# A two-layer streaming encoder step: layers written out in place of a loop, and buffers handed back without TensorE drains

## The reference

```
for l in range(2):
    h = rmsnorm(x, norm1_g[l])
    xa, ga, xq, q, k, v, gates = split(h @ w_in[l])
    ya = rg_lru(causal_conv(xa)) * gelu(ga)            # mixer A, a recurrence
    yb = pooled(xq) @ pool_w[l]                        # mixer B
    yc = diff_attention(rotary(q), rotary(k), v)       # mixer C, 8 heads, two softmaxes each
    g = sigmoid(gates)                                 # three gates
    m = g0 * (ya @ proj_a[l]) + g1 * (yb @ proj_b[l]) + g2 * (yc @ proj_c[l])
    x = x + m @ w_out[l]
    h2 = rmsnorm(x, norm2_g[l])
    s = scores of (h2 @ peer_wq[l]) against sub-keys   # 8 heads, 2 x 128 keys
    idx, gate = 16 best pairs of keys, softmax         # out of 16384 experts
    act = gelu(<h2, u[idx]>)                           # one neuron per expert
    x = x + sum(gate * act * v[idx])
y = rmsnorm(x, final_g)
```

## Time and profile before

| | |
|---|---|
| median of 3 runs | 2577.77 us (2577.13 to 2579.86) |
| the profiled execution | 2582.31 us, span from the first to the last instruction 2580.6 us, 38213 instructions |
| busy share of the span | TensorE 77% (weight loads 44%), VectorE 62%, GpSimd 30%, ScalarE 26% |
| granted TensorE clock, mean | 0.909 |
| DMA | 852.67 MB, mean 330 GB/s |

### The profile page before, as it was taken

How to read it: one execution, slowest core, us unless ns; L and a number is a source line. 1 busy time by engine, 2 the same in 40 slices (tenths; PEclk the granted TensorE clock), 3 DMA queues, 4 the chain that set the end, 5 groups by cost and what they waited for, 6 DMA issues and landing times.

```text
span 2580.6 us, 38213 instructions
## 1 busy us (share of the span) xinstructions
PE 1992.8 (77%) x11708; PEld 1135.9 (44%) x11708; DVE 1587.4 (62%) x4310; ACT 673.0 (26%) x1659; POOL 779.6 (30%) x831
## 2 busy tenths in 40 slices
PE   7999997888677666566689999888786776656666
PEld 5555786655334212111255557866553442111112
DVE  3544046565767788787535440556667678777785
ACT  2422113331323222222223230233312132222223
POOL 0122012232434344444201210132334443444341
PEclk9999999999888788888899999999998988787878
DMA  6124649999999999999741348499999999999996
GB/s 212 64 102 166 242 166 404 418 411 419 418 419 403 409 420 418 413 410 416 306 153 64 135 155 283 169 404 418 409 418 417 420 403 409 420 407 413 411 421 251
DMA packets 156818, 852.67 MB, mean 330 GB/s; under 512 B 19312, under 2 KB 39280, under 8 KB 72640
## 3 DMA queue, kind: packets, MB, share of 16 engines
q0 software_dynamic: 95280, 677.24, 63.8%
q1 hardware_dynamic: 61328, 172.89, 18.1%
HBM read 843.35 MB, written 6.71 MB: 329 GB/s over the span
## 4 chain that ended last, share of the span: by engine, by line
PE 24%; DMA 24%; issue 15%; DVE 13%; PEld 12%; PEldq 5%; DVEq 3%; ACT 2%; POOL 1%; ACTq 0%; POOLq 0%; SPq 0%
DMA W<-in_peer_uv_dram,IDX 9%; DMA MIX_RINGS<-in_peer_uv_dram,IDX 9%; PE ps L766 7%; DMA WQKV_E<-in_peer_uv_dram,IDX 5%; PEld ps L836 5%; PEldq L1031 4%; PE ps L1045 4%; PEld ps L1029 3%; PE ps L784 3%; DVE MIX_RINGS L1603 3%; DVEq L1442 2%; PEld ps L901 2%; PE ps L772 2%; DVE W L1603 1%; PEld ps L864 1%
## 5 line engine op out<-in xcount | busy, mean ns | idle before, releaser
L1029 PE MATMUL ps<-MIX_RINGS,GC 64*64 64x512 f32 x3712 | 637.7, 689 | 201.7 <-ACT GC L1248 155.0
L711 POOL DMA_INDIRECT MIX_RINGS<-in_peer_uv_dram,IDX x400 | 429.7, 1074 | 797.0 <-PEq L1031 443.8
L1029 PE MATMUL ps<-W,GC 64*64 64x512 f32 x1840 | 388.6, 718 | 242.4 <-ACT GC L1248 221.5
L1029 PEld LDWEIGHTS ps<-MIX_RINGS,GC 64*64 64x64 f32 x3712 | 182.3, 152 | 517.5 <-issue 517.5
L711 POOL DMA_INDIRECT W<-in_peer_uv_dram,IDX x182 | 203.7, 1119 | 448.9 <-PEq L1031 372.8
L1248 ACT ACTIVATE GC<-twins,WV 128x64 f32<-128x64 f32 x640 | 170.5, 336 | 569.1 <-DVEq L1616 562.5
L1603 DVE CUSTOM_DVE_ANT_0 MIX_RINGS<-MIX_RINGS 128x1024 f32<-128x1024 f32 x224 | 268.4, 1223 | 74.3 <-DMA MIX_RINGS<-in_peer_uv_dram,IDX 67.1
L1603 DVE CUSTOM_DVE_ANT_0 MIX_RINGS<-MIX_RINGS,WQKV_E 128x1024 f32<-128x1024 f32 x176 | 213.0, 1225 | 161.6 <-DMA MIX_RINGS<-in_peer_uv_dram,IDX 154.2
L1029 PEld LDWEIGHTS ps<-W,GC 64*64 64x64 f32 x1840 | 105.7, 154 | 444.1 <-issue 444.1
L1242 ACT ACTIVATE GV<-AV 128x4 f32<-128x4 f32 x160 | 32.9, 205 | 710.9 <-DVEq L1604 710.9
L1603 DVE CUSTOM_DVE_ANT_0 W<-W,MIX_RINGS 128x1024 f32<-128x1024 f32 x126 | 154.0, 1225 | 42.5 <-DMA W<-in_peer_uv_dram,IDX 31.4
(11 more groups left out here) (265 smaller groups left out, 2748.0 us busy)
## 6 DMA issues: line engine op xcount, KB each, us to landing
W<-in_merge_w_dram SPq DMA_DIRECT2D x40, 1024.0 KB, 4.9
W<-in_merge_w_dram SPq DMA_DIRECT2D x60, 512.0 KB, 13.7
WQKV_E<-in_qkv_w_dram SPq DMA_DIRECT2D x16, 1536.0 KB, 7.4
W<-in_query_w_dram SPq DMA_DIRECT2D x16, 1024.0 KB, 11.5
W<-in_w_in_dram SPq DMA_DIRECT2D x12, 1024.0 KB, 10.7
W<-in_query_w_dram SPq DMA_DIRECT2D x20, 512.0 KB, 9.1
W<-in_out_w_dram SPq DMA_DIRECT2D x8, 1024.0 KB, 14.5
MIX_RINGS<-in_peer_uv_dram,IDX POOLq DMA_INDIRECT x400, 13.6
```

The lines of the kernel that those rows point to most:

```text
L711: pool.indirect_dma_start(UV[r], None, table, bass.IndirectOffsetOnAxis(IDX[:, n % 2, j:j + 1], 0))\
L1029: pe.matmul(ps[o:o + CHUNK, n:n + 512], w[r, :], v[r, d * 512:(d + 1) * 512], start=False, stop=False, skip_group_check=True)
```

## The change

The loop over the layers becomes a Python loop, so that both layers are written out one after the other and every target of a wait is a constant. The fillers `nop(nofuse=True)` behind waits are taken out on all engines. TensorE's drains that gave buffers back go, except the ones in `experts` and at the layer's end; in their place the last matmul of the group counts the semaphore up, and semaphores that then say the same thing twice are merged into one (`ga_ps`, `pa_ps`, `cb_ps`, `xb_ps`, `cache_free` go; others wait on `w_used`, `half_used`, `att_done`). Two things more: in `first_queries` half of the `wqh_used` counts is replaced by `pq_ps`; and the square of the first tile ahead of the second norm is taken in four quarters as the additions to X finish, with ScalarE's root table loaded ahead, and summed by VectorE. The order of TensorE's work is the same as before. The cut diff shows one place of each kind, in the order gate, branches, chunk, rest_queries, head, experts and ff for TensorE, then ScalarE and VectorE.

```
-            with sp.Fori(0, DEPTH) as l:
+            for l in range(DEPTH):
...
                 sp.wait_ge(*layer_done.at(l, 0))
-                sp.nop(nofuse=True)
...
                         h = g * 2 + par
-                        sp.wait_ge(*cache_free.at(l, h - 1))
-                        sp.nop(nofuse=True)
+                        if g:
+                            sp.wait_ge(*att_done.at(l, h - 1))
...
                                   start=c == 0, stop=c == KC - 1)
-                i.then_inc(ga_ps.sem, 1)
-                pe.drain().then_inc(w_used[b].sem, 1)
+                i.then_inc(w_used[b].sem, 1)
...
-                pe.drain().then_inc(w_used[3].sem, 1)
+                i.then_inc(w_used[3].sem, 1)
...
-                i.then_inc(pa_ps.sem, 1)
-                pe.drain().then_inc(w_used[4].sem, 1)
+                i.then_inc(w_used[4].sem, 1)
...
                             .then_inc(half_used[4].sem, 1)
-                    pe.drain().then_inc(cb_ps.sem, 1)
...
-                i.then_inc(pq_ps.sem, 1)
-                pe.drain().then_inc(w_used[slot].sem, 1)
+                i.then_inc(w_used[slot].sem, 1)
...
                 pe.wait_ge(*rot_done.at(l, 2 * (3 * g + 2 * par + 1)))
-                pe.nop(nofuse=True)
                 pe.wait_ge(*ex_done.at(l, h * 2 * TILES))
-                pe.nop(nofuse=True)
...
                 i.then_inc(att_done.sem, 1)
-                pe.drain().then_inc(cache_free.sem, 1)
...
                     pe.wait_ge(*dg_ready.at(l, p + 2))
-                    pe.nop(nofuse=True)
...
-                        i.then_inc(ff_ps.sem, 1)
-                    pe.drain().then_inc(w_used[FF_SLOT[u]].sem, 1)
+                        i.then_inc((ff_ps, w_used[FF_SLOT[u]])[k].sem, 1)
...
-                act.wait_ge(*xa_ev.at(l, GB))
-                squares([0])
+                act.activation(LE[:, 0:1], eps_c[:, :], ACT.Sqrt)
+                for n in range(GB):
+                    act.wait_ge(*xa_ev.at(l, n + 1))
+                    i = act.activation(HN[0][:, n * UNIT:(n + 1) * UNIT], X[:, 0, n * UNIT:(n + 1) * UNIT], ACT.Square,
+                                       accum_out=ssq[:, n:n + 1])
+                act.drain().then_inc(sqa_done.sem, 1)
+                act.wait_ge(*ssa_ready.at(l, 1))
+                act.activation(sd[:, 0:1], ss[:, 0:1], ACT.Sqrt, bias=eps_c[:, :], scale=1.0 / D_MODEL)\
+                    .then_inc(sq_done.sem, 1)
...
-                fence()
+                dve.wait_ge(*sqa_done.at(l, 1))
+                dve.tensor_reduce(ss[:, 0:1], ssq[:, :], AX_X, ALU.add)
+                dve.drain().then_inc(ssa_ready.sem, 1)
                 normed(l, 1, 0)
```

More of the change, by code:

```diff
@@ L272, in build @@
         ss = sb("ss", [P, TILES])
+        ssq = sb("ssq", [P, GB])
         sd = sb("sd", [P, TILES])
@@ L397, in build @@
         wqh_in = landing("wqh_in", 2 * (PH - AHEAD))
-        wqh_used = signal("wqh_used", 2 * (PH - AHEAD))
-        pq_ps = signal("pq_ps", Q_BLOCKS)
+        wqh_used = signal("wqh_used", PH - AHEAD)
+        pq_ps = signal("pq_ps", PH)
         pq_ev = signal("pq_ev", Q_BLOCKS)
@@ L430, in scores, with chunk_done @@
             return a if t < 2 else a[0:DEC_SEQ]
+        def chunk_done(l, c):
+            return half_used[(3, 4)[c % 2]].at(l, c // 2 + 1)
         def bcast(row):
@@ L709, in gathers @@
                         pool.wait_ge(*uv_free.at(l, PREV[p] + 1))
-                    pool.nop(nofuse=True)
                     pool.indirect_dma_start(UV[r], None, table, bass.IndirectOffsetOnAxis(IDX[:, n % 2, j:j + 1], 0))\
                         .then_inc(uv_in[r].sem, 16)
-            with pool.Fori(0, DEPTH) as l:
+            for l in range(DEPTH):
                 for h in range(HEADS):
@@ L794, in branches @@
                     for c in range(RC):
-                        pe.matmul(two(bank(3 + b, 0, UNIT)), YT[:, b * RC + c, 0:P], W2[3][:, :, b * RC + c, :],
-                                  start=c == 0, stop=c == RC - 1)
-                pe.drain().then_inc(w_used[3].sem, 1)
+                        i = pe.matmul(two(bank(3 + b, 0, UNIT)), YT[:, b * RC + c, 0:P], W2[3][:, :, b * RC + c, :],
+                                      start=c == 0, stop=c == RC - 1)
+                i.then_inc(w_used[3].sem, 1)
                 pe.wait_ge(*w_in_slot[4].at(l, FF_USES[4] + u + 1))
@@ L865, in rest_output @@
                                       W2[u % 2][:, :, c, :], start=c == 0, stop=c == KC - 1)
-                i.then_inc(xb_ps.sem, 1)
-                pe.drain().then_inc(w_used[u % 2].sem, 1)
+                i.then_inc(w_used[u % 2].sem, 1)
             def first_queries(l, h, k):
@@ L883, in first_queries @@
                     i.then_inc(pq_ps.sem, 1)
-                if h >= AHEAD:
-                    pe.drain().then_inc(wqh_used.sem, 1)
+                elif h >= AHEAD:
+                    i.then_inc(wqh_used.sem, 1)
             def first_scores(l, h):
@@ L1033, in _ @@
             norm_turn(0, 0, range(TILES))
-            with pe.Fori(0, DEPTH) as l:
+            for l in range(DEPTH):
                 pe.wait_ge(*nt_ev.at(l, TILES * TURNS))
@@ L1253, in _ @@
             turned(0, 0, range(TILES))
-            with act.Fori(0, DEPTH) as l:
+            for l in range(DEPTH):
                 def ff(u):
@@ L1679, in _ @@
             dve.drain().then_inc(gain_used.sem, 1)
-            with dve.Fori(0, DEPTH) as l:
+            for l in range(DEPTH):
                 dve.wait_ge(*small_in.at(l, NSMALL))
```

80 lines of the change are left out of this document (12 added, 68 removed).

## The result

The changed kernel takes 2533.59 us (median of 4 runs, 2529.81 to 2534.49), the kernel before 2578.82 us beside it: a ratio of 0.982, 95% interval 0.9803 to 0.9837, 45.2 us less. The forecast was 2542, with 2527 to 2557 for 8 times in 10. The profiled execution took 2534.36 us, 48.0 less than that of before, where the steps added up to 35.9. So the direction and the kind were right, and a fifth to a quarter of the gain was missed. The profile says where.

What follows compares the result with a forecast made beforehand. DMA engines bound the gather stages (1797 us, unchanged); the other 784 us could shrink. Layers 31.6, turn 1.9 and tails 2.4 sum to 35.9 us off 2582.3, giving 2546.4, or 2542 at the runs' median; range 2527 to 2557.

Steps and rivals of the forecast that it cites:

- projections: Boundaries between projection units on TensorE, six a layer: removing the drains saves 2.45 us a layer.
- merge: Three rounds of gates, branch products and a turn on TensorE, 19.83 us each: 7.5 us a layer saved, at least 5.5.
- The squares: Second norm's square taken in quarters: norm 1.6 us earlier, but counted as nothing because TensorE's first chunk ends as late.
- The turn: Turn of the loop between layers: without TensorE's branch 1.9 us saved once, 0.9 to 3.5 depending on the clock.
- the heads: First to last head on TensorE: 4.0 us a layer saved, at six boundaries of 0.6 each and in single waits.
- The seventh boundary: Last boundary between heads: no gain, as TensorE waits 1.80 us for VectorE's copy of K in any case.
- the wait for ScalarE's copy: TensorE's wait in each head for the turned weights: 0.05 to 0.1 us saved, eight times, 0.4 a layer.
- Gather stages: Stages of 899 and 898 us with DMA engines always busy: unchanged within 5 us, only starting earlier.
- More than forecast: Rival, chance 0.16: squares give 3.2, earlier clock 1.6, single waits and tails some 4; gain 45 us, 2533.
- The next one is late: Rival, chance 0.20: other engines hold up the heads and the merge keeps half its crossings; gain 24.7 us, 2553.
- No effect: Rival, chance 0.04: drains only stood for the matmuls' own completion time, boundaries keep their idle; gain 4 us, 2574.
- Slower: Rival, chance 0.05: straight code makes TensorE wait for instructions, up to 4.15 us a packet; fifteen packets give 2604 us.

## Why the prediction was right, and where it was short

**Right in mechanism and size.** The matmuls' pace read from an undisturbed row carried the two largest blocks: projections 2.45 against 2.90 and 2.91 (3.45 less the clock's 0.54), merge 7.5 against 7.84 and 7.91. TensorE's drains are left in the experts and at the layer's end alone, units and rounds are as long as forecast, and the weights were in time. The squares gave nothing for the reason given, the chunk in front of the turn, and the runs with and without that cover show it twice. The turn gave 1.9 by the removed branch (2.03 to 0.1 behind the evacuation) and about 0.5 of the clock, within the 0.9 to 3.5 that was allowed for.

**Short: the heads, 4.0 against 6.02 and 6.19, the one large miss.** It lies beyond the sum's own upper ends for them (3.8 and 0.8). A boundary gained 0.65 on average, close to the 0.6 forecast. Two other steps failed. The seventh boundary was put at nothing, since TensorE waits 1.80 us for VectorE's copy there anyway; it gained 0.71 like the others, and the wait stayed (1.81). VectorE copies what the transposes behind that very boundary wrote, so its copy came earlier by the same amount. And the wait for ScalarE's copy was put at 0.05 to 0.1 a head for the filler's 51 ns, but measured 0.15, and 0.06 more went ahead of the scores: 1.5 a layer, where 0.4 was taken. Seven times 0.65 and 0.21 are 6.0.

**Right in sum, wrong in parts.** At the boundary the text gave the price to "a drain and two waits" without saying which. The runs do: 0.29 the drain; 0.11 the fillers, but behind a drain only; 0.2 the register instructions, behind a drain only. The few hundredths that are left of the 0.65 may be the counts that were merged (1.18 on average with all three back, 1.23 before); no run takes them alone. The Trainium skill, "Perfetto Trace Analysis", section "Identifying Dependency Chains", says that an instruction that waits for several engines may get semaphore instructions put in front of it. The trace agrees: of the two waits at each head's start the changed kernel has one semaphore instruction left, 51 ns in the median. The price that the prediction set against it, 0.1 a boundary, is nothing here, since 0.58 is the same with one or with both.

**Not in the sum.** Up to the first projection 1.41 came off, 0.92 of it because X landed earlier in that execution: ScalarE starts on it at 9.17 us in the profile before and 8.25 in that after, and anywhere from 8.1 to 9.3 in the other runs, whatever was changed. It is scatter, and part of why the profiled pair shows 48.0 and the medians 45.2. From the turn of the normed tile to the first gather 0.61 and 0.92 came off, which was not counted: in layer 0 VectorE's choice of the first experts takes 10.73 us from its first copy (340.12) to the first gather (350.85), where before it took 11.34.

**Gather stages.** They were to start earlier and stay as they were. By the first and last gather they shrank by 3.3 and 3.0 us (891.2 to 887.9, 887.7 to 884.7), of which the tail behind them gives some back. In the four executions with the loop they are 890.8 to 893.6 in layer 0, in the others 886.0 to 890.5, the longest of these with drains and fillers; in layer 1 that one's 888.4 lies among those with the loop, 887.4 to 889.2. With the DMA share at 1.00 and 1.01 the bytes still set most of the length. That waits add some us to it is likely by these figures, but with one profiled execution of each kernel it is not shown, nor by which instruction.

**The rivals.** *More than forecast* had the nearest time, 2533, for other reasons: the squares gave nothing, the clock behind the turn 0.5 of the 1.6 that it had, and the heads, of which it named only the single waits, the most. *The next one is late* failed: the merge's weights and GpSimd's rotation had the slack. *No effect* is out: the idle pieces went with the drains, and gates start 3.45 us apart, and 3.92 with the drains back. *Slower* by waits for instructions: no such stall on TensorE's chain was found, and fewer packets were fetched for straight code than for the loop, 163 where before had 210.

## What to carry to other kernels

Before putting an edit at nothing because its engine waits for another one there, look at what that other engine was waiting for: if it is fed from behind the edit, the wait moves along and the gain is kept. A drain is dear twice: by itself, 0.29 us at a boundary of heads, and by the waits, fillers and register instructions behind it, which cost nothing there without a drain and another 0.3 with one. So take drain and waits out together, and price them together. A part that is covered by other work, like the squares here, is worth its time only when the cover is moved too, which 16 matmuls placed later did.

## What was not expected of the hardware

A step's price depends on what stands ahead of it: at the heads' boundary two waits with fillers and register instructions cost TensorE 0 us behind matmuls, and 0.3 us behind a drain. And kernels with the same program of TensorE in a stretch differ by some 3.6 us there by the granted clock (0.94 and 0.98 from the last head to the output product), as much as some of the edits that were to be measured.
